# First feed-forward up projection of a two-block transformer in fp32: eight block products per pair of tiles against seven, with weight block sums kept in DRAM

## The reference, cut to what matters

```
xn = rms_norm(h, norm_gains[layer, 2])
u = causal_depthwise_conv(xn @ w_up[layer], conv_w[layer], conv_b[layer])   # 3 taps along the tokens
u_gate, u_val = jnp.split(u, 2, axis=-1)                                     # 2816 channels each
ffn = (jax.nn.gelu(u_gate, approximate=True) * u_val) @ w_down[layer]
```

## Time and profile before

| | |
|---|---|
| median of 3 runs (lowest to highest) | 1528.55 us (1528.21 to 1529.2) |
| the profiled execution's own time | 1527.86 us |
| its span, first to last instruction | 1526.1 us |
| PE busy, matmul | 1478.5 us (97%) |
| DVE busy | 1037.5 us (68%) |
| ACT busy | 654.6 us (43%) |
| moved by DMA | 147.75 MB, mean 97 GB/s |

### The profile page before, as it was taken

One profiled execution on the slowest core, in us unless ns is written; L12 is line 12 of the kernel. 1 busy time (PEld: TensorE's weight loads), 2 busy tenths in 40 slices (PEclk: granted clock), 3 DMA queues, 4 the chain that ended last, 5 costly groups with the idle time before them and its releaser, 6 DMA issues.

```text
span 1526.1 us, 27858 instructions
## 1 busy us (share of the span) xinstructions
PE 1478.5 (97%) x11729; PEld 1302.8 (85%) x11729; DVE 1037.5 (68%) x1481; ACT 654.6 (43%) x1052; POOL 23.8 (2%) x21
## 2 busy tenths in 40 slices
PE   9999999999999999999999899999989999999998
PEld 7988778889998999999788667768667999998876
DVE  5544458874547977777665776676778888885444
ACT  5343434343344222222343455546645555554353
POOL 0000000000000000000000020000000000000000
PEclk9999999999999999999999999999999999999999
DMA  5130124452322332232444212110113233322222
GB/s 187 57 135 29 43 74 137 158 164 79 125 84 77 114 129 105 104 132 77 147 152 157 70 60 101 56 36 28 43 42 111 84 111 112 111 98 83 86 94 83
DMA packets 37709, 147.75 MB, mean 97 GB/s; under 512 B 4177, under 2 KB 4433, under 8 KB 27857
## 3 DMA queue, kind: packets, MB, share of 16 engines
q1 hardware_dynamic: 36288, 142.76, 27.1%
q10 hardware_dynamic: 1152, 2.16, 0.4%
q0 software_dynamic: 144, 1.05, 0.2%
HBM read 143.86 MB, written 2.10 MB: 96 GB/s over the span
## 4 chain that ended last, share of the span: by engine, by line
PE 81%; DVE 10%; ACT 5%; issue 3%; DMA 1%; POOL 0%; ACTq 0%; DVEq 0%; SPq 0%
PE ps L601 18%; PE ps L602 18%; PE ps L603 18%; PE ps L1557 4%; PE ps L1558 4%; PE ps L1559 4%; DVE t L2332 2%; ACT t L1608 2%; PE ps L637 1%; PE ps L638 1%; PE ps L639 1%; PE ps L1263 1%; PE ps L1232 1%; PE ps L825 1%; DMA t<-in_XT 1%
## 5 line engine op out<-in xcount | busy, mean ns | idle before, releaser
L601 PE MATMUL ps<-t 128*128 128x258 f32 (+3 forms) x2144 | 683.4, 319 | 15.6 <-DVE t L2640 4.3
L602 PE MATMUL ps<-t 128*128 128x258 f32 (+3 forms) x2144 | 672.8, 314 | 0.0
L603 PE MATMUL ps<-t 128*128 128x258 f32 (+3 forms) x2144 | 672.6, 314 | 0.0
L601 PEld LDWEIGHTS ps<-t 128*128 128x128 f32 x2144 | 405.5, 189 | 60.1 <-issue 17.1
L603 PEld LDWEIGHTS ps<-t 128*128 128x128 f32 x2144 | 405.5, 189 | 26.1
L602 PEld LDWEIGHTS ps<-t 128*128 128x128 f32 x2144 | 405.2, 189 | 23.0
L2332 DVE TENSOR_TENSOR t<-t 128x1024 fp32r<-128x1024 f32 (+2 forms) x120 | 205.6, 1713 | 202.4 <-ACT t L1608 202.3
L1608 ACT ACTIVATE t<-t 128x1024 fp32r<-128x1024 f32 (+2 forms) x120 | 173.8, 1448 | 186.0 <-PE ps L603 171.7
L1557 PE MATMUL ps<-t 128*128 128x256 f32 x504 | 141.8, 281 | 0.1
L1559 PE MATMUL ps<-t 128*128 128x256 f32 x504 | 141.8, 281 | 0.0
L1558 PE MATMUL ps<-t 128*128 128x256 f32 x504 | 141.8, 281 | 0.0
(11 more groups left out here) (332 smaller groups left out, 1744.7 us busy)
## 6 DMA issues: line engine op xcount, KB each, us to landing
t<-in_W SPq DMA_DIRECT2D x74, 1024.0 KB, 4.8
t<-in_W SPq DMA_DIRECT2D x62, 512.0 KB, 3.3
t<-in_W SPq DMA_DIRECT2D x100, 256.0 KB, 3.6
t<-in_W SPq DMA_DIRECT2D x4, 644.0 KB, 3.7
t<-in_XT ACTq DMA_DIRECT2D x8, 264.0 KB, 8.4
out<-t SPq DMA_DIRECT2D x8, 256.0 KB, 2.7
t<-in_W SPq DMA_DIRECT2D x1, 1056.0 KB, 4.9
t<-in_ROPE POOLq DMA_DIRECT2D x1, 1024.0 KB, 5.2
```

Source lines behind the costliest of these rows:

```text
L601: pe.matmul(out, wh, xh, start=first, stop=False)
L602: pe.matmul(out, wh, xl, start=False, stop=False)
L603: return pe.matmul(out, wl, xh, start=False, stop=last)
```

## The change

From the eighth pair on (15 of 22), gate and value are made together by seven block products: per pair 7 x 4 (depth blocks) x 3 = 84 matmuls of 258 columns. The blocks are halves in depth and halves in tokens. For this:

- Three sums of weight blocks per pair and one in place (`up_sums`, four DVE operations on 128 x 512) are made in the first attention. SP loads the raw chunk of a pair (1 MB) into a spare buffer (`sums_load`), DVE adds, SP stores the buffer to DRAM (`sums_store`, 1 MB), and the next load into the same buffer waits until the store has landed. These DMAs stand in SP's queue between the weight loads, the sums in DVE's queue between its other work.
- In the up stage SP loads the seven blocks in four parts from the weights and from DRAM (`up_load`); ACT and DVE split them by parts (`up_high`, `up_low`), ACT keeps four partial results (`up_keep`), DVE adds them (`up_gather`, two per pair).
- The inputs' sums and their high and low parts are made in the plain pairs (`z_tile`, `b_high`, `b_low`, `turn_sum`, `turn_high`, `turn_low`). The inputs of the fast pairs have the norm's scale in them.
- The first tap of the convolution goes from DVE to ACT for all pairs (`first_tap`, Identity with scale and bias).
- The 22 conditioning pieces of the up stage go to the down stage, which then has 48 (2 or 3 per chunk).
- The rope table's load goes from POOL's queue to SP's.
- After the last fast pair, the first two splits of activations for the down projection (`narrow`) come after the last `up_gather`.

```diff
@@ SP's queue
             for n in range(2, AT["ga", 0] + 2):
                 weights(n)
+                if n == 2:
+                    sums_load(0)
+                    sums_load(1)
+                if 4 <= n <= 8:
+                    sums_store(n - 4)
+                    sums_load(n - 2)
+                if n == 9:
+                    for i in (5, 6, 7):
+                        sums_store(i)
+                        sums_load(i + 2)
+                if n == 10:
+                    sums_store(8)
+                    sums_load(10)
+                if n == 11:
+                    for i in (9, 10, 11, 12):
+                        sums_store(i)
+                        sums_load(i + 2)
+                if n == 13:
+                    sums_store(13)
+                    sums_store(14)
...
+            def sums_load(i):
+                at, width = W_AT["up", PLAIN_UP + i]
+                if i >= 2:
+                    sp_.wait_ge(S[f"d_h{2 + i % 2}"], sums_landed(i - 2))
...
+            def sums_store(i):
+                sp_.wait_ge(S["gu_x"], 4 * i + 4)
...
@@ DVE's queue, start and first attention
             split(3)
+            up_sums(0)
             norm0(4, 8)
             evac_qk(4)
             split(4)
+            up_sums(1)
             evac_qk(5)
             evac_qk(6)
             split(AT["va", 0] + 1)
+            up_sums(2)
             evac_qk(7)
...
                 evac_v(0, i)
+                if i in (0, 2):
+                    up_sums(3 + i // 2)
                 if i == 6:
                     split(AT["va", 1] + 1)
+                if i == 8:
+                    up_sums(5)
...
+SUM_UNITS = {1: 6, 2: 7, 4: 8, 6: 9, 8: 10, 10: 11, 12: 12, 15: 13, 17: 14}
                     fox_least(n)
                     fill_a(n, 0)
+                    if n in SUM_UNITS:
+                        up_sums(SUM_UNITS[n], (0, 1))
                     fox_normalise(n)
                     fill_a(n, 1)
...
+                if n in SUM_UNITS:
+                    up_sums(SUM_UNITS[n], (2, 3))
@@ ACT's queue, up stage, pair 7 + f
+            for f in range(FAST_UP):
+                i = PLAIN_UP + f
+                up_keep(f, 0)
+                if f >= 1:
+                    first_tap(2 * i - 1)
+                if f + 1 < FAST_UP:
+                    up_high(f + 1, 0)
+                else:
+                    split(AT["down", 0])
+                up_keep(f, 1)
+                up_keep(f, 2)
+                if f + 1 < FAST_UP:
+                    up_high(f + 1, 1)
+                    up_high(f + 1, 2)
+                first_tap(2 * i)
+                if f + 1 < FAST_UP:
+                    up_high(f + 1, 3)
+                gelu(i)
+                up_keep(f, 3)
+            narrow(0, 0, dh1, aF, "up_a")
+            narrow(0, 1, dh1, aF, "up_a")
+            first_tap(43)
@@ DVE's queue, up stage
+            for j in range(2 * PLAIN_UP):
...
+                if j == 2 * PLAIN_UP - 1:
+                    up_low(0, 0)
+            for f in range(FAST_UP):
+                i = PLAIN_UP + f
+                if f >= 1:
+                    up_gather(f - 1, 1)
+                if f + 1 < FAST_UP and f >= 1:
+                    up_low(f + 1, 0)
...
+                taps(2 * i - 1)
+                gated(i - 1)
...
+                if f + 1 < FAST_UP:
+                    up_low(f + 1, 1)
+                up_gather(f, 0)
+                if f + 1 < FAST_UP:
+                    up_low(f + 1, 2)
+                taps(2 * i)
+                if f + 1 < FAST_UP:
+                    up_low(f + 1, 3)
+            up_gather(FAST_UP - 1, 1)
+            narrow(0, 0, dh1, dl1, aF)
+            narrow(0, 1, dh1, dl1, aF)
+            taps(43)
+            gated(21)
@@ PE's queue, one block product
+                out = bank(4 * ((f + PLAIN_UP) % 2) + (3, 0, 1, 3, 1, 2, 3)[b], 258)
+                pe.wait_ge(S["w_lo"], up_split(7 * f + b))
+                if b == 0:
+                    pe.wait_ge(S["up_c"], 2 * PLAIN_UP + 2 * f - 2)
+                if b in (3, 4, 6):
+                    pe.wait_ge(S["keep"], 4 * f + {3: 1, 4: 2, 6: 3}[b])
```

More of the change, by code:

```diff
@@ L122, with up_used, up_place, up_runs @@
 FAST_PART = (0, 0, 1, 1, 2, 3, 3)
+def up_used(i):
+    return 2 * PLAIN_UP - 2 if i < 4 else 2 * PLAIN_UP if i < 8 else 2 * PLAIN_UP + i - 7
+def up_place(f, b):
+    return (7 * f + b + 4 * (UP0 % 2)) % 8
+def up_runs(f, bs):
+    return [bs] if up_place(f, bs[0]) + len(bs) <= 8 else [[b] for b in bs]
+def up_blocks(part):
+    return [b for b in range(7) if FAST_PART[b] == part]
+def up_loads(f, part):
+    return [[b] for b in up_blocks(part)] if part == 3 else up_runs(f, up_blocks(part))
+def up_landed(f, part):
+    first = 16 + (16 * len(range(f % 2, FAST_UP, 2)) if part < 2 else 0)
+    return first + 16 * sum(len(up_loads(e, part)) for e in range(f % 2, f + 1, 2))
+def whole(n):
+    return 16 * len([m for m in range(n % 2, n + 1, 2) if not UP0 <= m < UP0 + FAST_UP])
+def sums_landed(i):
+    return 16 + 16 * (i // 2 + 1)
 def fast_done(f, b):
@@ L317, in build @@
         fxmn, fxrs, fxri = (sb(s_foxw, [P, 36]) for _ in range(3))
+        sb(s_foxw, [P, 192])
+        ub = [sb(s_foxw, [P, 4, 512]) for _ in range(2)]
         s_foxw.close()
@@ L546, in _ @@
                 weights(n)
-            for i in range(22):
+            for i in range(PLAIN_UP - 2):
                 weights(AT["up", i] + 2)
-                for a in ADA_UP[i]:
-                    ada(a)
+            for f in range(FAST_UP):
+                for part in range(4):
+                    up_load(f, part)
+            for i in range(2):
+                weights(AT["down", i])
             for c in range(22):
@@ L1914, in narrow, with first_tap @@
                 ac.activation(ah[v % 4][:, :], src[:, v % 22, :], ACT.Copy).then_inc(S["an_hi"], 1)
-            for i in range(22):
-                if i > 2:
-                    split(AT["up", i] + 1)
-                if i == 21:
-                    narrow(0, 0, dh1, aF, "up_a")
-                    narrow(0, 1, dh1, aF, "up_a")
+            def first_tap(j):
+                i, part = j // 2, j % 2
+                col = i + 22 * part
+                if i >= 1:
+                    ac.wait_ge(S["up_a"], i)
+                ac.wait_ge(S["up_c"], j + 1)
+                ac.activation(uu[part][:, :], uc[part][:, 4:TQ], ACT.Identity, bias=V("cb", col), scale=V("cw", 3 * col + 2)
+                              ).then_inc(S["up_t"], 1)
@@ new lines, in up_keep @@
+            def up_keep(f, part):
+                b, dst = ((3, up_k[0][:, 0:258]), (1, up_k[1][:, 258:TQ]), (3, up_k[0][:, 258:TQ]), (3, up_k[1][:, 0:258]))[part]
+                if part < 2:
+                    ac.wait_ge(S["up_c"], 2 * PLAIN_UP + 2 * f - 1 + part)
+                ac.wait_ge(S["mm_up"], 2 * PLAIN_UP + 7 * f + (1, 3, 4, 7)[part])
+                ac.activation(dst, bank(4 * ((f + PLAIN_UP) % 2) + b, 258), ACT.Copy).then_inc(S["keep"], 1)
+            for i in range(PLAIN_UP):
@@ L1922, in _ @@
                 if i == 1:
                     split(AT["up", 3])
-                ac.wait_ge(S["up_u"], 6 * i + 3)
-                ac.activation(uu[0][:, :], uu[0][:, :], ACT.Gelu_apprx_tanh).then_inc(S["up_gl"], 1)
+                if 2 < i < PLAIN_UP - 1:
+                    split(AT["up", i] + 1)
+                first_tap(2 * i)
+                if i == 2:
+                    for k in range(4):
+                        b_high(k)
+                if i == 3:
+                    for k in range(4, 8):
+                        b_high(k)
@@ L2668, in _, with taps @@
             dv.wait_ge(S["rst"], 3)
-            for j in range(44):
+            def taps(j):
+                part, u, c = j % 2, uu[j % 2], uc[j % 2]
+                col = j // 2 + 22 * part
+                for q in range(2):
+                    if q == 0:
+                        dv.wait_ge(S["up_t"], j + 1)
+                    else:
+                        dv.wait_ge(S["up_u"], 2 * j + 1)
+                    dv.scalar_tensor_tensor(out=u[:, :], in0=c[:, 3 - q:TQ - 1 - q], scalar=V("cw", 3 * col + 1 - q), in1=u[:, :],
+                                            op0=ALU.mult, op1=ALU.add).then_inc(S["up_u"], 1)
```

339 lines of the change are left out of this document (246 added, 93 removed).

## The result

The changed kernel takes 1576.04 us (median of 4 runs, 1575.16 to 1576.32), the kernel before 1528.38 us (4 runs, 1528.1 to 1529.2). The ratio is 1.031, with a 95% interval from 1.0292 to 1.0328: 3.1% slower. The forecast, 1552 with a range of 1537 to 1564, had the sign right and the size wrong by half: 24 us of loss forecast, 48 measured.

The account below looks back on a forecast made before the run. PE was taken to bound the kernel (81% of the chain, DVE 10%). From 1527.9 us, 26.1 lost in attention less 2.6 gained in the up stage gave 1551.4, or 1552 as median; range 1537 to 1564.

Parts of the forecast that it names:

- table rival: Up stage: ACT switches tables between Identity and gelu, two loads of 1.28 us per pair; 1590 us, chance 0.02.
- hidden case: First attention: sums' loads not held behind the weights' waits, little DVE time shows; 1520 us as middle, chance 0.10.
- First value step: First attention: DVE's first sums delay the evacuation that the first value step needs; 3.7 us lost.
- Fourth sum: First attention: load 4 waits behind weights 6 and store 2, delaying the forget gates; 13.0 us lost.
- slow-store rival: Attention: a 1 MB store takes 10 us, so three stores ahead of DVE or ACT cost more; 1562 us, chance 0.15.
- Clock and units 0 to 2: First attention: half clock behind the fourth sum's stop, 1.8 us, plus late sums and loads in units 0 to 2, 1.5.
- Chunk 12 and the rest: Attention: chunk 12 late behind store 12 and load 14, 4.7 us, plus sums in units 12 and 15, 1.4.
- The loop: Up stage's fast pairs: gather, tap, high and low halves between DVE and ACT set 10.87 us per pair, 13 times.
- Entry and exit: Fast pairs' ends: 17.0 us from last plain tile to the loop's first gather, 11.0 from last-but-one gather to down projection.
- Clock at the ends: Up stage: PE's waits of 3.6 and 4 us at entry and exit may cost its clock, 0 to 3.6, taken as 1.
- products set the pace: Up stage: DVE and ACT keep up, so a fast pair takes 10.11 us; 1541 us, chance 0.18.
- table rule: Up stage: about 2.7 us per ACT table switch, adding 5.4 us per pair if Identity were outside the gelu's set.

Follow-up runs that it names:

- run 2: Changed kernel with only SP's queue order altered, stores and loads of early sums ahead of weights: 1553.10 us (one run).
- run 3: Changed kernel with the sums' loads and stores issued from POOL's queue instead of SP's: 1551.74 us (one run).
- run 4: Changed kernel with ACT making the next pair's first high half ahead of the odd tile's first tap in fast pairs: 1558.01 us (one run).
- run 6: Changed kernel with sums placed later in DVE's queue and SP's stores, loads and weights reordered: 1560.84 us (one run).
- run 5: On top of run 4, queue orders changed at the up stage's entry, plain pairs and exit: 1554.38 us (one run).
- run 10: Changed kernel with sums later and spread over units, transfers in POOL's queue, up stage reordered, separate buffers for narrowed activations: 1514.10 us, ratio 0.9903.

## Why the forecast was wrong, step by step

**The mechanisms stood.** The first value step came at 64.3 as forecast. The stop at the fourth sum, its cause in SP's order, the half clock behind it, chunk 12, pairs by a loop and not by products, 3.4 and 3.9 us of idle PE at the ends of the fast stage: all are there, and the main causes were taken away one by one, each with its loss: SP's order (run 2), chunk 12 (run 3), the loop (run 4), the late first value step (run 6). The table rival and the hidden case are out. What failed are terms of the sum that were too small or missing, nearly all in one direction: a store beside a load, the clock behind each stop, the waits for loads 6 and 7, the first tap, and the plain pairs.

**The attention side** was forecast at 26.1 us and lost 40.3:

- *First value step:* 3.7 forecast, 4.1 measured. But PE's 3.63 us there cost its clock as well (0.50 from 64.3 to 70.0), 2.6 us more by the time chunk 6 is issued. I had charged the clock behind the big stop alone, though in the kernel before 3.85 us of idle had already cost it (and the line below). This term was left out.

```profile
460.38 0.55 PE L601 MATMUL ps<-t 128*128 128x258 f32 x1 [3.85 <-DVE t L2640]
```

- *Fourth sum:* 13.0 forecast; 15.3 measured (22.0 less 6.7). The term "a load and a store take 6.7 us" failed: chunk 6 went out at 81.22 and store 2 had landed at 90.26, 8.67 us after its own issue and 9.0 after chunk 6's. The 6.7 was read from two loads, and from the end of their traffic; the second of them landed 7.2 us after the first's issue. In the stretch from 60 to 130 us the five stores have a median of 8.7; alone a store takes 3.8 to 4.5. The slow-store rival was therefore true in company and false alone. With 9.0 for 6.7 the step comes to 15.3.
- *Clock and units 0 to 2:* 1.8 + 1.5 = 3.3 forecast, 7.6 measured, and 2.9 more up to unit 4. The step "load 6 lands 3 us after DVE wants it, load 7 is hidden" failed. DVE waited 5.29 and 8.45 us for these loads, since each came behind a store that took 8.4 to 10.4 us; PE stopped for 4.27 and 1.62 us, the first with half the clock for another 5.5 us.
- *Units 4 to 14:* nothing forecast, nothing lost (32.5 to 32.5).
- *Chunk 12 and the rest:* 4.7 + 1.4 = 6.1 forecast, 7.8 measured; again PE's stop of 6.13 us took the clock with it (0.51 from 229.4 to 234.0).

Two errors, then, make most of the difference of 14.2: a store beside a load does not land as early as a second load would, which moved the fourth sum and loads 6 and 7; and each stop from 3.6 us up cost its clock here, not the largest alone.

**The up side** was forecast to give 2.6 us and lost 7.7:

- *The loop:* 13 x 10.87 = 141.3 forecast, 755.34 - 608.53 = 146.8 measured, 11.29 a pair. In the pair shown, 11.25 us, the first tap makes 0.17 of the 0.38 us too much: it took 0.81 and not the 0.73 of the earlier trace rows, and stands in the loop twice. That price was of an activation with one column, its scale; the tap has two, scale and bias (the gelu, with none, took 0.63). The rest is handovers: the tap starts 0.78 us after the gather (0.72 taken), twice, and `gated` 1.56 after the taps begin (1.46 taken). Small terms of 0.1, times 13 pairs, made 5.5 us.
- *Entry and exit:* 17.0 and 11.0 forecast, 17.8 and 12.1 measured.
- *Plain pairs:* costed at 0, and 1.3 us lost in all; PE waited 0.71 and 1.17 us for DVE's split, which waited for ACT: ACT's high half stands behind a gelu that now waits for taps made one tile later. My sum had no row for these pairs at all.
- *Clock at the ends:* the forecast took 1 us for both stops together. Behind the one at the down projection alone it was 0.59 over 7 us, 2.9 us lost. That is most of the 4.3 us that the down stage lost; two of PE's sums of conditioning columns also moved there from the up stage. I did not take the rest apart. 1.1 us came back behind the stage, where a stop of 1.70 us of the kernel before is gone.

Of the rivals, *products set the pace* was wrong for the kernel as changed, and right for run 4: its 10.11 us is what a pair takes once two instructions change places.

On the table rule, the trace now answers: first taps and gelus alternate in 15 pairs with one table load of 1.28 us in front of all. The Trainium skill (ScalarE: Activation LUTs, Table sets: the hidden batching unit) says that cheap functions, identity among them, are in every set; for the gelu's set the trace agrees, and for others no run shows it.

## What to carry to other kernels

Work moved to where an engine is idle is priced by the queues that its transfers pass through, not by the engine alone: the same sums cost 41.7 us as first placed and 5.9 in another queue and at other places, and 22.9 of that came from the order of stores and weights in one queue. Give such transfers a queue with nothing else in it, leave a buffer the time that store and load take when they run together, and price a transfer by what runs beside it. And in a loop that goes back and forth between two engines, look at what stands ahead of the instruction that the other engine waits for; moving one instruction was worth 15 us in the pairs here.

## What was not expected of the hardware

- In the changed kernel a 1 MB store landed in 3.8 to 4.5 us alone, in 6.2 when issued 1.6 us behind a load, and in 8.4 to 10.6 us when issued right behind one or two loads. Two loads do better: in the kernel before, those issued at 74.48 and 74.91 had both landed 7.2 us after the first issue, where one alone takes 4.8; a load and a store took 9.0, about what the two take one after the other. Three loads issued from 217.30 to 218.22 in the changed kernel took 10.0. Why a store beside a load is dearer than a load is open.
- In the changed kernel each of the attention's stops of PE from 3.6 to 15.1 us was followed by busy time at a granted clock of 0.50 to 0.61, and in all traces together none of the 44 stops of 3.6 us or more had a mean above 0.66 in the 4 us behind it. Below that it is open. The same stop of 3.44 us in the entry cost nothing in run 2 (first line) and half the clock for 4 us in run 3 (second); one of 2.05 us cost the clock in run 5 (0.61 over 3.8 us) and nothing in run 10 (third and fourth); and one of 1.75 us in run 10 was followed by 0.57 over 4 us.

```profile
570.80:574.80 4.00, 4.00 (x33) 1.00 0.58 168
570.70:574.70 4.00, 4.00 (x18) 0.50 0.53 164
559.60:561.70 2.10, 0.05 (x1) 1.00 1.01 344
561.70:566.00 4.30, 4.30 (x36) 1.00 0.36 103
```

- The loads of the sums took 6.6 us (median) from POOL's queue in run 3 where they took 5.1 from SP's in the changed kernel, but in other company. Those with nothing beside them took 5.0 to 5.2 from POOL's and 4.6 to 4.8 from SP's, stores 4.1 to 4.2 for 3.8 to 3.9, so the queue itself is worth some 0.3 us of it.
